# Holding each expert's weight loads back until the expert before has landed, in a one-layer hybrid block with 64 experts

## The chip, the cores and the metric

The kernel runs on one core of a Trainium2 chip. The metric is the device time of one execution in microseconds, the median of several. The core has TensorE (matmuls and transposes), VectorE, ScalarE, GpSimd and SyncE (SP), which issues DMAs; 16 DMA engines move data between HBM and the on-chip memory (SBUF). Engines run their own instruction streams and meet at semaphores.

## What is computed

One decoder layer over 512 tokens of width 1024, all in float32: an input projection, a spatial gating branch and an attention branch, an output projection, then a mixture of experts, and a gated per-layer embedding. The part that matters here is the mixture of experts:

```python
# t: 512 x 1024 tokens; 64 experts, hidden width 256, each token goes to 8 experts
scores = jax.nn.sigmoid((t @ w_router).astype(jnp.float32))
...
_, eidx = lax.top_k(jnp.where(emask, sel, -jnp.inf), TOP_K)
...
y = (jax.nn.silu(t @ w_sh_gate) * (t @ w_sh_up)) @ w_sh_down
for g in range(N_GROUPS):
    sl = slice(g * EXPERTS_PER_GROUP, (g + 1) * EXPERTS_PER_GROUP)
    a = jax.nn.silu(jnp.einsum('td,edf->tef', t, w_gate[sl])) * jnp.einsum('td,edf->tef', t, w_up[sl])
    y = y + jnp.einsum('tef,efd->td', a * combine[:, sl, None], w_down[sl])
```

The gate and up weights of one expert are 1024 x 256 each, the down weights 256 x 1024: three transfers of 1 MB for each of 64 experts.

## The kernel before

The projections and both branches come first, then the router and the shared expert, then a loop over the 64 experts, and a tail that sums eight expert rows for each token and applies the last gate.

**The expert loop.** Each expert handles up to 104 rows at once. GpSimd gathers its token rows from HBM by an indirect DMA (L621, `ya<-h_rows,gidx`, two buffers), TensorE transposes them (L1796), and runs gate and up as one product (L1767, L1775 to L1777), and the down product (L1811 to L1813). ScalarE and VectorE split each weight into a high and a low part before TensorE reads it (ScalarE L916 and VectorE L1370 for gate and up, ScalarE L935 and VectorE L1388 for down). GpSimd scatters the results back to HBM (L640, `expert_rows<-ya,sidx`). On TensorE step j does the gate and up product of expert j, the transposes of expert j+1 and the down product of expert j-1.

**The weight ring.** Weights lie in `arena`, a ring of `RING` = 4 slots; slot r holds gate, up and down of expert e with e mod 4 = r. All weight loads are issued by SP, on one queue, in program order. `expert_gu(e, r)` issues the gate and the up load (L422), and both count up the semaphore `w_gu[r]` by 16 as they land; `expert_dn(e, r)` issues the down load (L427) with `w_dn[r]`. Each of the 16 DMA engines moves its part of every transfer and adds 1. ScalarE waits for `w_gu` and `w_dn` before it splits a weight. SP loads experts 0 to 3 ahead of the loop. For experts 4 to 63 it waits for room: `gu_done`, which TensorE counts up after each gate and up product, and `dn_done`, after each down product:

```python
with sp.Fori(1, E // RING) as q:
    for r in range(RING):
        sp.wait_ge(gu_done, q * RING + (r - RING + 1))
        expert_gu(q * RING + r, r, one=False)
        sp.wait_ge(dn_done, q * RING + (r - RING + 1))
        expert_dn(q * RING + r, r, one=False)
```

With e = 4q + r, the gate and up loads of e wait until expert e-4 has left the products, and its down load until the down product of e-4 is done. Nothing on SP waits for a landing. As the down product of e-4 comes in TensorE's step e-3, after the gate and up product of e-3, one release lets three loads go together: down of e, gate and up of e+1. A second copy of this loop, L465 to L472, is for passes after the first.

Of the kernel before, what the change touches and what calls it, by code (L numbers as in the profile page):

```python
# [6 lines left out]
def hybrid_block_kernel(nc, a, out):  # L7
# [37 lines left out]
    E = a["w_router"].shape[2]  # L45
# [10 lines left out]
    RING = 4  # L56
# [12 lines left out]
    with ctx:  # L69
# [11 lines left out]
        def sem(name):  # L81
            return ctx.enter_context(nc.semaphore(name))
# [23 lines left out]
        def take(n):  # L106
# [73 lines left out]
              for i in range(2)]  # L180
# [34 lines left out]
        ROWS = [("positions", NT), ("g_mix", KD), ("g_ple_in", KD), ("sgu_b", G), ("mla_g_qa", KQ),  # L215
                ("mla_g_kva", KKV), ("qk_g_q_nope", 1), ("qk_g_k_nope", 1)]
        NROW = sum(n for _, n in ROWS)
        col = {}
        for name, n in ROWS:
            first = sum(len_ for _, len_ in ROWS[:len(col)])  # L220
            col[name] = sm[:, first:first + n]
# [58 lines left out]
        rt_logit, rt_score, m_ready = sem("rt_logit"), sem("rt_score"), sem("m_ready")  # L280
        rk_done, ks_done, rank_ready, R_ready, nb_ready = sem("rk_done"), sem("ks_done"), sem("rank_ready"), sem("R_ready"), sem("nb_ready")
        sh_gu, sh_silu, sh_a, sh_at, sh_aT, sh_dn, sh_y = (sem(f"sh_{n}") for n in ("gu", "silu", "a", "at", "aT", "dn", "y"))
        held = sem("held")
        xg_zero = sem("xg_zero")
        w_gu = [sem(f"w_gu{r}") for r in range(RING)]
        w_dn = [sem(f"w_dn{r}") for r in range(RING)]
# [77 lines left out]
        def _(sp):  # L364
# [54 lines left out]
            def expert_gu(e, r, one=True):  # L419
                for g, name in enumerate(("w_exp_gate", "w_exp_up")):  # L420
                    src = a[name][0][e] if one else a[name][0][bass.ds(e, 1)].rearrange("o d f -> (o d) f")
                    sp.dma_start(arena[:, r * WEXP + g * KD * FF:r * WEXP + (g + 1) * KD * FF],  # L422
                                 src.rearrange("(p k) f -> p (k f)", p=P)).then_inc(w_gu[r], 16)

            def expert_dn(e, r, one=True):
                src = a["w_exp_down"][0][e] if one else a["w_exp_down"][0][bass.ds(e, 1)].rearrange("o d f -> (o d) f")
                sp.dma_start(arena[:, r * WEXP + WGU:(r + 1) * WEXP],  # L427
                             src.rearrange("(p k) f -> p (k f)", p=P)).then_inc(w_dn[r], 16)
# [28 lines left out]
            with sp.Fori(1, E // RING) as q:  # L457
                for r in range(RING):
                    sp.wait_ge(gu_done, q * RING + (r - RING + 1))
                    expert_gu(q * RING + r, r, one=False)  # L460
                    sp.wait_ge(dn_done, q * RING + (r - RING + 1))
                    expert_dn(q * RING + r, r, one=False)
            sp.wait_ge(nb_ready, 1)
            n_pass = sp.value_load(nb_i, min_val=1, max_val=NPASS_MAX)
            with sp.If(n_pass > 1):  # L465
                with sp.Fori(1, n_pass) as b:
                    with sp.Fori(0, E // RING) as q:
                        for r in range(RING):
                            sp.wait_ge(gu_done, b * E + q * RING + (r - RING + 1))
                            expert_gu(q * RING + r, r, one=False)  # L470
                            sp.wait_ge(dn_done, b * E + q * RING + (r - RING + 1))
                            expert_dn(q * RING + r, r, one=False)  # L472

            sp.wait_ge(gate_room, n_pass)
# [1403 lines left out]
```

## Time and profile before

| | |
|---|---|
| median of 3 runs | 1344.4 us (1340.31 to 1345.1) |
| the profiled execution | 1339.67 us, of which span 1337.9 us |
| TensorE busy | 1197.0 us, 89% of the span |
| VectorE busy | 869.1 us, 65% |
| ScalarE busy | 720.0 us, 54% |
| GpSimd busy | 295.8 us, 22% |
| moved by DMA | 302.91 MB, mean 226 GB/s |

The span runs from the first to the last instruction of one execution taken by the profiler. Busy shares are averages over stages with different limits. The expert loop fills the time from about 540 to about 1225 us.

### The profile page before, as it was taken

The numbers are of one execution on the slowest core, as the hardware profiler recorded it, in microseconds if no ns is written. First come the engines' busy times: TensorE is split into PE (matmuls) and PEld (weight loads), VectorE is DVE, ScalarE is ACT, GpSimd is POOL, SyncE is SP. The second block draws the span as 40 slices with busy tenths as digits, with TensorE's granted clock in tenths as the row PEclk, the third lists the DMA queues.
The fourth block names the chain that finished last, engine by engine and source line by source line (L and its number), as shares of the span: only waits on it lengthen the run. The fifth ranks groups of instructions, "written<-read, shape, count | busy, mean of one in ns | idle before, by whom it ended". The sixth has DMA issues, their size and how long they took to land.

```text
span 1337.9 us, 17977 instructions
## 1 busy us (share of the span) xinstructions
PE 1197.0 (89%) x5569; PEld 901.7 (67%) x5569; DVE 869.1 (65%) x1379; ACT 720.0 (54%) x1270; POOL 295.8 (22%) x309
## 2 busy tenths in 40 slices
PE   6996999998999998999999999999999999996258
PEld 6984788685667844677777677666667766664246
DVE  5356342385443354888888778777787888775974
ACT  5542242374432240677677666666776767665223
POOL 2015000060551001122222112212221221112640
PEclk9997999998999999899999999999999999998579
DMA  6332112023002474499999999999999999985741
GB/s 208 126 114 75 63 63 81 20 81 142 1 1 79 156 300 157 181 343 343 352 352 333 341 338 349 344 338 332 339 344 335 337 335 338 343 294 209 325 199 48
DMA packets 71756, 302.91 MB, mean 226 GB/s; under 512 B 15107, under 2 KB 20262, under 8 KB 45734
## 3 DMA queue, kind: packets, MB, share of 16 engines
q1 hardware_dynamic: 51846, 264.64, 54.5%
q0 software_dynamic: 19296, 35.69, 8.1%
q10 hardware_dynamic: 576, 2.10, 0.4%
q8 instruction: 21, 0.34, 0.1%
q14 instruction: 17, 0.14, 0.0%
HBM read 290.64 MB, written 33.55 MB: 242 GB/s over the span
## 4 chain that ended last, share of the span: by engine, by line
PE 48%; DMA 30%; DVE 11%; issue 5%; ACT 4%; POOL 1%; SPq 1%; DVEq 0%; POOLq 0%; ACTq 0%
DMA arena<-in_w_exp_up 18%; DMA ya<-h_rows,gidx 11%; PE bank L1483 7%; PE bank L1518 5%; PE bank L1519 5%; PE bank L1522 5%; DVE resid L1433 2%; PE bank L1475 2%; PE bank L1796 2%; PE bank L1586 2%; DVE arena_r L1388 2%; PE bank L1767 2%; PE bank L1671 2%; PE bank L1583 1%; PE bank L1603 1%
## 5 line engine op out<-in xcount | busy, mean ns | idle before, releaser
L1370 DVE TENSOR_TENSOR arena_r<-arena,win_r 128x1024 fp32r<-128x1024 f32 x192 | 223.6, 1220 | 88.4 <-ACT win_r L916 88.3
L916 ACT ACTIVATE win_r<-arena 128x1024 fp32r<-128x1024 f32 x192 | 189.7, 1060 | 149.7 <-DMA arena<-in_w_exp_up 139.0
L640 POOL DMA_INDIRECT expert_rows<-ya,sidx x64 | 71.9, 1123 | 508.0 <-DVE gidx L1329 479.3
L1775 PE MATMUL bank<-win_r,work_r 128*128 128x512 f32 x384 | 176.8, 460 | 0.0
L1388 DVE TENSOR_TENSOR arena_r<-arena,hT_r 128x1024 fp32r<-128x1024 f32 x128 | 150.8, 1219 | 12.0 <-ACT hT_r L935 11.9
L1776 PE MATMUL bank<-win_r 128*128 128x512 f32 x384 | 150.1, 391 | 0.0
L1777 PE MATMUL bank<-arena_r,work_r 128*128 128x512 f32 x384 | 150.0, 391 | 0.0
L1518 PE MATMUL bank<-arena_r,hT_r 128*128 128x512 f32 (+2 forms) x320 | 123.6, 386 | 12.4 <-DVE win_r L1029 12.4
L935 ACT ACTIVATE hT_r<-arena 128x1024 fp32r<-128x1024 f32 x128 | 129.2, 1071 | 0.0
L1767 PE MATMUL bank<-arena,work 128*128 128x512 f32 x256 | 122.8, 602 | 1.6 <-ACT work L926 1.6
L1519 PE MATMUL bank<-arena_r 128*128 128x512 f32 (+2 forms) x320 | 122.3, 382 | 0.0
L1522 PE MATMUL bank<-win_r,hT_r 128*128 128x512 f32 (+2 forms) x320 | 122.0, 381 | 0.0
L1811 PE MATMUL bank<-hT_r,work_r 128*128 128x512 f32 x256 | 106.4, 416 | 1.8 <-DVE work_r L1363 1.8
L1029 DVE SCALAR_TENSOR_TENSOR win_r<-win,small,arena_r 128x512 fp32r<-128x512 f32 (+2 forms) x80 | 67.2, 909 | 62.3 <-ACT arena_r L693 62.3
L1813 PE MATMUL bank<-arena_r,work_r 128*128 128x512 f32 x256 | 101.1, 395 | 0.0
L1812 PE MATMUL bank<-hT_r,work_r 128*128 128x512 f32 x256 | 100.1, 391 | 0.0
L621 POOL DMA_INDIRECT ya<-h_rows,gidx x66 | 81.8, 1240 | 60.7 <-DVE gidx L1329 40.1
L1796 PE MATMUL bank<-ident,ya 128*128 128x128 f32 x512 | 70.5, 281 | 27.1 <-DMA ya<-h_rows,gidx 27.0
L1775 PEld LDWEIGHTS bank<-win_r,work_r 128*128 128x128 f32 x384 | 72.5, 189 | 28.6 <-issue 15.6
L1776 PEld LDWEIGHTS bank<-win_r 128*128 128x128 f32 x384 | 72.5, 189 | 28.6 <-issue 15.6
L1777 PEld LDWEIGHTS bank<-arena_r,work_r 128*128 128x128 f32 x384 | 72.2, 188 | 16.0
L1518 PEld LDWEIGHTS bank<-arena_r,hT_r 128*128 128x128 f32 x320 | 61.3, 191 | 26.4 <-DVE win_r L1029 16.5
(280 smaller groups left out, 2233.6 us busy)
## 6 DMA issues: line engine op xcount, KB each, us to landing
arena<-in_w_exp_gate SPq DMA_DIRECT2D x64, 1024.0 KB, 10.7
arena<-in_w_exp_up SPq DMA_DIRECT2D x64, 1024.0 KB, 25.1
arena<-in_w_exp_down SPq DMA_DIRECT2D x64, 1024.0 KB, 18.6
win<-in_w_in SPq DMA_DIRECT2D x8, 2048.0 KB, 7.7
arena<-expert_rows SPq DMA_DIRECT2D x8, 2048.0 KB, 11.9
win<-in_w_o SPq DMA_DIRECT2D x2, 2048.0 KB, 7.7
arena<-in_w_ple_gate SPq DMA_DIRECT2D x2, 2048.0 KB, 17.4
win<-in_mla_w_qb SPq DMA_DIRECT2D x4, 576.0 KB, 4.0
```

The lines of the kernel that those rows point to most:

```text
L916: act.activation(gu_hi[n % 2][:, :, cols], gu_w[n % RING][:, :, cols], ACT.Copy).then_inc(gu_hi_r, 1)
L935: act.activation(wdn_hi[j % 2][:, k, :], wdn[j % RING][:, k, :], ACT.Copy).then_inc(dn_hi, 1)
L1370: dve.tensor_tensor(gu_lo[n % RING][:, :, cols], gu_w[n % RING][:, :, cols], gu_hi[n % 2][:, :, cols].bitcast(F32), ALU.subtract).then_inc ...
L1388: dve.tensor_tensor(wdn_lo[j % RING][:, k, :], wdn[j % RING][:, k, :], wdn_hi[j % 2][:, k, :].bitcast(F32), ALU.subtract).then_inc(dn_lo, 1)
L1518: pe.matmul(b_, x_hi, w_hi, start=(k == 0), stop=False)
L1519: last = pe.matmul(b_, x_lo, w_hi, start=False, stop=False)
L1522: last = pe.matmul(b_, x_hi, w_lo, start=False, stop=(k == KD - 1))
L1767: pe.matmul(b_, x_f[:, k - KS, :], wgu[j % RING][:, k], start=(k == KS), stop=False)
L1775: pe.matmul(b_, x_hi[:, k, :], w_hi, start=False, stop=False)
L1776: pe.matmul(b_, x_lo[:, k, :], w_hi, start=False, stop=False)
L1777: last = pe.matmul(b_, x_hi[:, k, :], gu_lo[j % RING][:, :, k * FF:(k + 1) * FF], start=False, stop=(k == KS - 1))
L1811: pe.matmul(b_, hi, w_hi, start=(k == 0), stop=False)
```

## The change

SP's loop gets two more waits for each expert. Before the gate and up loads of expert e it waits until those of e-1 have landed (`w_gu` of the slot before, 32 counts for each use of the slot), and before the down load of e until that of e-1 has landed (`w_dn`, 16 counts). The waits for room stay. Between the two waits stands a count on a new semaphore, `room_seen`, for which nobody waits. When a load is issued, at most one down load (before gate and up), or one gate and one up load (before down), can still be on its way, so that at most three are outstanding. The same edit is made in the loop for further passes, which is cut here.

```diff
-        held = sem("held")
+        held, room_seen = sem("held"), sem("room_seen")
...
             with sp.Fori(1, E // RING) as q:
                 for r in range(RING):
                     sp.wait_ge(gu_done, q * RING + (r - RING + 1))
+                    sp.sem_inc(room_seen, 1)
+                    sp.wait_ge(w_gu[(r - 1) % RING], q * 32 + 32 * (r > 0))
                     expert_gu(q * RING + r, r, one=False)
                     sp.wait_ge(dn_done, q * RING + (r - RING + 1))
+                    sp.sem_inc(room_seen, 1)
+                    sp.wait_ge(w_dn[(r - 1) % RING], q * 16 + 16 * (r > 0))
                     expert_dn(q * RING + r, r, one=False)
```

On SP's stream at the start of the loop body (slot 0, then the start of slot 1) the rows are these. REGISTER_ALU and ISA are small instructions of the sequencer that carry the waits; `w_gu3` and `w_dn3` are the semaphores of slot 3, which holds the expert before.

```order
 L457 UNCONDITIONAL_BRANCH
 L457 ISA
-L422 ISA [waits gu_done]
+L461 REGISTER_ALU [waits gu_done]
+L422 ISA [waits w_gu3]
 L422 DMA arena<-in_w_exp_gate 128x2048
 L422 DMA arena<-in_w_exp_up 128x2048
-L427 DMA arena<-in_w_exp_down 128x2048 [waits dn_done]
+L465 REGISTER_ALU [waits dn_done]
+L427 DMA arena<-in_w_exp_down 128x2048 [waits w_dn3]
 L459 REGISTER_ALU
```

The order of the three loads is as it was; each wait for room now stands on an instruction of its own, and the wait for the landing behind it. On the same stream in slots 2 and 3 of the loop body:

```order
+L422 ISA [waits gu_done,w_gu1]
 L422 DMA arena<-in_w_exp_gate 128x2048
 L422 DMA arena<-in_w_exp_up 128x2048
-L427 DMA arena<-in_w_exp_down 128x2048 [waits dn_done]
-L422 ISA [waits gu_done]
+L427 DMA arena<-in_w_exp_down 128x2048 [waits dn_done,w_dn1]
+L422 ISA [waits gu_done,w_gu2]
```

Here both waits stand on the same instruction; no load has moved past another.

## Rows read from the trace of the kernel before

**Rows 1.** The page: the span, and the chain that ended last, by line.

```profile
span 1337.9 us, 17977 instructions
...
DMA arena<-in_w_exp_up 18%; DMA ya<-h_rows,gidx 11%; PE bank L1483 7%; PE bank L1518 5%; PE bank L1519 5%; PE bank L1522 5%; DVE resid L1433 2%; PE bank L1475 2%; PE bank L1796 2%; PE bank L1586 2%; DVE arena_r L1388 2%; PE bank L1767 2%; PE bank L1671 2%; PE bank L1583 1%; PE bank L1603 1%
```

**Rows 2.** Stretches: us, busy time (x count) by engine, granted clock, DMA share, GB/s.

```profile
546.80:734.60 187.80, 181.37 (x876) 136.78 (x875) 156.57 (x238) 137.91 (x221) 44.23 (x35) 1.00 0.94 336
734.60:1179.80 445.20, 414.86 (x1970) 308.47 (x1969) 349.26 (x534) 305.29 (x493) 94.48 (x82) 1.00 0.95 339
```

**Rows 3.** SP's own waits, 735 to 1191 us: total, times, longest.

```profile
SPq L427 <- PE bank L1813: 388.8, 42, 12.1
```

**Rows 4.** Up loads of experts 4, 6, 22, 22 to 63, and 63: issue, landing.

```profile
L422 SPq DMA_DIRECT2D arena<-in_w_exp_up x1: 376/376/376, 547.2 to 547.2; - x1
...
DMA to landing us min/median/max: 7.4/7.4/7.4
...
L422 SPq DMA_DIRECT2D arena<-in_w_exp_up x1: 381/381/381, 569.5 to 569.5; - x1
...
DMA to landing us min/median/max: 13.6/13.6/13.6
...
735.06 26.79 DMA arena<-in_w_exp_up
...
DMA to landing us min/median/max: 23.5/26.0/28.0
...
L422 SPq DMA_DIRECT2D arena<-in_w_exp_up x1: 381/381/381, 1180.3 to 1180.3; - x1
...
DMA to landing us min/median/max: 25.9/25.9/25.9
```

**Rows 5.** Waits of the engines, 734 to 1181 us: total, times, longest.

```profile
ACT win_r L916 <- DMA arena<-in_w_exp_up: 125.7, 41, 5.1
```

**Rows 6.** Gate loads, from issue to the 16th count: expert 4, experts 22 to 63.

```profile
DMA to landing us min/median/max: 4.8/4.8/4.8
...
DMA to landing us min/median/max: 9.6/10.7/14.0
```

**Rows 7.** The chain at a landing, and SP's next issue in the timeline.

```profile
1227.61 3.84 DMA expert_rows<-ya,sidx
...
1231.52 0.82 SPq L487 DMA_DIRECT2D arena<-expert_rows  x2
```

**Rows 8.** Issues and landings: up 38; down 4, down 21 to 63, down 38.

```profile
909.00 0.38 SPq L422 DMA_DIRECT2D arena<-in_w_exp_up  x1
...
DMA to landing us min/median/max: 27.5/27.5/27.5
...
DMA to landing us min/median/max: 5.5/5.5/5.5
...
DMA to landing us min/median/max: 16.4/19.3/20.1
...
919.59 0.33 SPq L427 DMA_DIRECT2D arena<-in_w_exp_down  x1
...
DMA to landing us min/median/max: 19.2/19.2/19.2
```

**Rows 9.** Gathers (L621), issue to landing: at 553.3, 572 to 735, 734 to 1181 us.

```profile
DMA to landing us min/median/max: 6.0/6.0/6.0
...
DMA to landing us min/median/max: 12.0/12.8/13.2
...
DMA to landing us min/median/max: 10.6/12.3/13.2
```

**Rows 10.** The chain in the first stretch: start us, us, what.

```profile
696.35 13.19 DMA ya<-h_rows,gidx
...
717.48 12.63 DMA ya<-h_rows,gidx
```

More of the change, by code:

```diff
@@ L469, in _ @@
                             sp.wait_ge(gu_done, b * E + q * RING + (r - RING + 1))
+                            sp.sem_inc(room_seen, 1)
+                            sp.wait_ge(w_gu[(r - 1) % RING], b * (32 * E // RING) + q * 32 + 32 * (r > 0))
                             expert_gu(q * RING + r, r, one=False)
                             sp.wait_ge(dn_done, b * E + q * RING + (r - RING + 1))
+                            sp.sem_inc(room_seen, 1)
+                            sp.wait_ge(w_dn[(r - 1) % RING], b * (16 * E // RING) + q * 16 + 16 * (r > 0))
                             expert_dn(q * RING + r, r, one=False)
```

## The prediction

> **What bounds the kernel now.** I begin with the page. The chain that ended last is nearly one half TensorE, but the one wait in it that is worth more than a matmul line is the landing of the experts' up weights, 18% of the span, with the gather of token rows next at 11% [rows 1]. Both lie in the loop over 64 experts. So the second view is the table of stretches over that loop, cut at the issue of experts 4, 22 and 63 (gate loads at 546.8, 734.6 and 1179.8 us). In the first stretch 18 experts go by in 187.8 us, 10.43 us each, in the second 41 in 445.2 us, 10.86 us each. TensorE is busy 181.37 / 18 = 10.08 and 414.86 / 41 = 10.12 us per expert, at a granted clock of 1.00 in both, which is the 2.4 GHz level. The DMA engines are busy 94 to 95% of both stretches [rows 2]. Two resources stand almost level, and the loop goes from one pace to another along the way. The question is which of them sets the second pace.
>
> The waits seem to speak for TensorE: in the second stretch SP stands 388.8 us, 42 times, at L427, until TensorE has finished the down product of four experts back [rows 3]. SP is never late; it waits for room. But a wait for room tells nothing of where the things that fill the room are. That is in the landings. Expert 4's up load, issued at 547.2, lands 7.4 us later; expert 6's, at 569.5, after 13.6; expert 22's, at 735.06, after 26.79; from there on the median is 26.0, and the last one, at 1180.3, takes 25.9 [rows 4]. In the first stretch the weights are issued every 10.43 us and pile up in the queues. From the landings themselves: 583.1 (569.5 + 13.6) to 761.9 for experts 6 to 22 is 11.2 us each, and 761.9 to 1206.2 for experts 22 to 63 is 10.84 us each. So the transfers land at about 11 us per expert all along. TensorE was ahead for some 18 experts, used up the four-slot ring, and has gone at the transfers' pace since. ScalarE confirms it, as it waits 125.7 us in 41 times for the up load in the second stretch, 3.1 us per expert [rows 5]. Queued weights, not slots or TensorE, bound the loop.
>
> One more thing must be read from the landings. The gate load is issued just ahead of the up load and shares its semaphore, and what stands as its landing is the 16th of 32 counts. In an empty queue it comes after 4.8 us and in the steady loop after 10.7 [rows 6], when the up load's last count needs 26.0 more or less. Engines that went in step would put one transfer of some 3 us between the two. So a part of the 16 DMA engines has done its share some 15 us before the rest: the load is bound by a few laggards, whose queues never run dry, while the quick ones wait for the next issue.
>
> **The change, part by part.** For each of the 60 experts of SP's loop two waits and two counts on SP are added; no transfer, byte, tile or compute instruction changes. SP stands in waits for nearly nine tenths of the second stretch (388.8 of 445.2 us), so the instructions themselves cost nothing; if SP's time ever counted, they would be under the 0.4 us that a load's issue takes [rows 4], and the gap below allows 0.3 us for them. Behind the waiting instruction on SP's queue stand only the later weight loads and, after the last, the load of the last gate's weights and of the expert rows. GpSimd's gathers and scatters have their own queue and pass.
>
> Which of the two waits will come last? Room is given three experts before the need: expert 38's up load is issued at 909.00 and lands 27.5 us later, at 936.5, when expert 35's slot is long free. So in the bound state the new wait ends last and SP issues by landings. The gate and up loads of e go out when those of e-1 have landed, with the down load of e-1 still in flight; the down load of e goes out when that of e-1 has landed, with gate and up of e in flight. The order of transfers on each DMA engine stays the same. The depth falls from the 26 us of work that lay ahead of a new load to one to three transfers.
>
> The laggards decide. Does their queue run dry? What must be covered is the way from the last count of the up load, through SP, to the first bytes of the next. SP reacts at once: the scatter's landing at 1227.61 + 3.84 = 1231.45 lets an SP load go at 1231.52 [rows 7]. For issue, first byte and receipt I take the lightly loaded rows: gate landed after 4.8 us [rows 6] and the up load behind it at 547.2 + 7.4 = 554.6, which is 3.0 us later, so 4.8 - 3.0 = 1.8 us is fixed; a lone down load takes 5.5 us [rows 8], and 5.5 - 3.0 = 2.5. With 0.3 us for SP the gap to cover is 2.1 to 2.8 us (an estimate from these rows). The cover at the tighter of the two places is the one down load still queued. It lands after its up load by 919.59 + 19.2 - 936.5 = 2.3 us at expert 38 [rows 8], and by the medians 10.6 + 19.3 - 26.0 = 3.9 us; a third of 10.84 is 3.6. At the other place two transfers cover, some 7 us, and nothing is lost.
>
> So the price per expert lies between 0 (2.1 against 3.9) and 0.5 us (2.8 against 2.3). A second effect lies inside this: backlogs average out when one engine or another is late, and the landings do scatter, 23.5 to 28.0 us for the up load around 26.0 [rows 4]; with a depth of one transfer each such delay makes all the others wait. Against it, the laggards have other work in a gap: a gather takes 12.8 and 12.3 us to land under weights and 6.0 us with almost none in flight [rows 9], so for most of each period rows of gathers and scatters are pending and can use a gap. I take a loss of 0.25 us at one expert in three, 0.08 us on average, nearer to the low end, since the medians clear the gap; 58 experts x 0.08 = 4.6 us. All else is kept: early on, experts 4 and 5 find the queues as empty as now; the tail after the last landing at 1206.2, 131.7 us, has the same work; TensorE's 10.1 us per expert lie beside the transfers.
>
> A rule of the Trainium skill speaks against the change: DMA: Bandwidth & Descriptors, section "Anatomy of one DMA", puts a fixed cost of about 2.0 us on a transfer, most of it until the write is confirmed, and a transfer held for a landing pays it in series. The rows above show 1.8 to 2.5 us, so trace and page agree; by the page's 2.0 alone the cover of 2.3 to 3.9 us would hold and the price be nil.
>
> **Sum.** The profiled execution took 1339.7 us (span 1337.9 and 1.8 around it), the median of the three runs is 1344.4. 1339.7 + 4.6 = 1344.3 for such an execution, 1344.4 + 4.6 = 1349 against the median.
>
> **The rivals.**
>
> (a) The queues do run dry (slower). It is the same mechanism at the high price: a gap at every expert. At 0.5 us it is 58 x 0.5 = 29 us, 1373 us. It decides from the point where the way from landing to first byte exceeds the time that the laggard has left in its down load, about 3.2 us on average between 2.3 and 3.9. For it: the scatter of the landings, and that only one transfer covers. Against it: medians and the pending gather rows. If the cover failed altogether, it would be 58 x 2.5 = 145 us; I see nothing for that, as the down load is always behind.
>
> (b) A shallow queue makes the laggards or the gathers quicker (faster). Gathers count too: in the first stretch the chain runs through gathers of 13.19 and 12.63 us, one per two experts, 696.35 to 717.48 being 21.1 us [rows 10]. If the weights fell under 10.43 us per expert, the loop would run at the first stretch's pace to its end: 41 x (10.86 - 10.43) = 18 us, 1327 us; if the gathers shortened too, TensorE's 10.1 would be next, 59 x 0.33 = 19 us more, 1307 us. For it: the gather's 6.0 against 12.8. Against it: the laggards are never without weights in either version, the same bytes pass, and the landings' pace was already 11.2 us when the depth was still 13.6 us, no better than at 26. A word of the skill bears on the gathers: the same page's section "Queues, rings and completion order" says that an engine takes turns between queue rows a packet at a time, by which a gather would wait for the neighbour's turn at any depth and not get quicker; no row here shows turns, and the chances don't use it.
>
> (c) The wait never ends last, so nothing changes: 1344. That would need landings earlier than room. Only at experts 4 to 6 is that so.
>
> **How the numbers follow.** What a measurement of this kernel can tell from no change is about 0.5%, 6.7 us. My forecast of about 1349 (0 to 0.11 us per expert) has 0.42 together with (c), which is 0.02 of it. Losses above that, to 0.5 us, 1351 to 1373, have 0.30, and beyond 0.06. Gains, (b), have 0.22: 0.14 down to 1325 and 0.08 beyond. The range takes the forecast, (a) to a little over its 0.5 us and (b) as far as 18 us: 1324 to 1374; outside are 0.08 + 0.06 and some slack. The likeliest case alone is 1340 to 1351. Faster 0.22, same 0.42, slower 0.36.
>
> **What the profile after would show.** SP's waits move: from L427 on TensorE's L1813 to waits on the up and down loads. The up load's issue-to-landing falls from 26 to about 10 us (11 less what SP waits), the down load's to about 10 too, and gate's 16th count comes 1 to 3 us, not 15, before the up load's last. The distance between issues stays 10.8 to 11.0 us in the second stretch; 11.3 would be rival (a), 10.4 rival (b). ScalarE still waits some 3 us per expert for the up load. The gathers stay above 11 us; under 9 speaks for (b). DMA busy share stays 93 to 95%; under 91% is (a). The forecast is wrong if the laggards are not the same few engines all along, since then a shared stop at each landing costs what the backlog now hides, or if a deep backlog itself slows them.

## The result

The changed kernel takes 1368.52 us (median of 4 runs, 1362.5 to 1373.34) against 1342.36 us before (4 runs, 1340.15 to 1345.1). The ratio is 1.0192, 95% interval 1.0142 to 1.0242: 26 us slower. That lies inside the stated range but outside the forecast of about 1349; it falls in the zone of rival (a), 1351 to 1373.

The page of the changed kernel, span and the chain that ended last, by line:

```profile
span 1368.9 us, 18157 instructions
...
DMA arena<-in_w_exp_up 47%; PE bank L1491 7%; PE bank L1526 5%; PE bank L1527 5%; PE bank L1530 5%; DVE resid L1441 2%; PE bank L1483 2%; PE bank L1594 2%; SPq L422 2%; PE bank L1679 2%; PE bank L1591 2%; PE bank L1611 1%; DVE arena_r L1436 1%; DVE win_r L1037 1%; PE bank L1602 1%
```

The landing of up weights was 18% of the chain [rows 1] and is 47% now. The gathers, 11% before, are gone from it. The table of stretches, cut at the same issues as in [rows 2] (gate loads of experts 4, 22 and 63):

```profile
551.10:760.90 209.80, 197.14 (x942) 146.56 (x941) 166.94 (x256) 145.14 (x236) 45.44 (x39) 1.00 0.89 316
760.90:1224.10 463.20, 420.87 (x1969) 309.73 (x1968) 348.81 (x532) 304.37 (x493) 92.74 (x83) 0.99 0.92 325
```

An expert takes 209.8 / 18 = 11.66 us and 463.2 / 41 = 11.30 us; it was 10.43 and 10.86. The last two columns matter: the DMA engines are busy 0.89 and 0.92 of the time instead of 0.94 and 0.95, and move fewer GB/s. So more of their time is idle than before. SP's waits in the second stretch, where [rows 3] had 388.8 us for room:

```profile
SPq L422 <- DMA arena<-in_w_exp_up: 327.7, 42, 10.3
SPq L427 <- DMA arena<-in_w_exp_down: 60.2, 38, 3.6
```

SP never waits for room there. From issue to landing in the same stretch, in this order up, gate (16th count), down, gather (L629) and scatter (L648):

```profile
DMA to landing us min/median/max: 8.3/10.7/12.6
...
DMA to landing us min/median/max: 5.3/7.5/9.0
...
DMA to landing us min/median/max: 8.5/11.2/14.5
...
DMA to landing us min/median/max: 6.6/10.6/14.1
...
DMA to landing us min/median/max: 4.6/6.7/11.1
```

The queues are as shallow as the change says: the up load lands after 10.7 us instead of 26.0. The gather comes down from 12.3 to 10.6 us.

The trace also has the time of each single count. For experts 24 to 61 (38 of them, medians of each rank), the 16 counts of a down load come in the kernel before at 5.2 to 5.7 us after its issue for the first eight, and then at 6.4, 9.3, 11.1, 11.5, 13.9, 16.5, 18.8 and 19.3 us. So half of the DMA engines have next to no backlog, and the other half has one of very unequal length. In the changed kernel the 16 counts come between 8.1 and 11.2 us. From gate's 16th count to the up load's last it is 15.9 us before and 3.4 us in the changed kernel.

**Where the 31 us of the two profiled executions lie** (1370.64 and 1339.67). Expert 4's gate load is issued at 551.1 instead of 546.8, so 4.3 us were lost before the loop. Of these, 3.1 us are SP's wait at L433, ahead of all expert loads, which is 92.4 us here and 89.3 us before. They are not the change's: in the experiments' profiles, whose code is the same up to there, this wait lies anywhere between the two. The other 1.2 us were not traced. From the landing of expert 4's up weights to that of expert 63's it is 558.8 to 1236.4 against 554.6 to 1206.2, 677.6 against 651.6 us: 26.0 us, 0.44 us for each of 59 experts. After that 132.5 against 131.7. The loss is the loop's, and it is spread over all of it.

### The profile page after: what moved, and what is told of

The parts are those of the page before. It is cut to its first block, busy times and chain, and to the rows that moved or that the text cites. A ratio compares the mean times of both kernels' runs of the same rounds, so it can differ in the third digit from the quotient of the medians.

```text
span 1368.9 us, 18157 instructions
## 1 busy us (share of the span) xinstructions
PE 1207.8 (88%) x5569; PEld 904.3 (66%) x5569; DVE 868.7 (63%) x1379; ACT 717.5 (52%) x1270; POOL 290.9 (21%) x309
## 4 chain that ended last, share of the span: by engine, by line
DMA 47%; PE 38%; DVE 8%; SPq 2%; issue 2%; ACT 2%; POOL 1%; ACTq 0%; DVEq 0%; POOLq 0%
DMA arena<-in_w_exp_up 47%; PE bank L1491 7%; PE bank L1526 5%; PE bank L1527 5%; PE bank L1530 5%; DVE resid L1441 2%; PE bank L1483 2%; PE bank L1594 2%; SPq L422 2%; PE bank L1679 2%; PE bank L1591 2%; PE bank L1611 1%; DVE arena_r L1436 1%; DVE win_r L1037 1%; PE bank L1602 1%
## 5 line engine op out<-in xcount | busy, mean ns | idle before, releaser
L648 POOL DMA_INDIRECT expert_rows<-ya,sidx x64 | 72.1, 1127 | 538.0 <-DVE gidx L1337 495.8
L1784 PEld LDWEIGHTS bank<-win_r 128*128 128x128 f32 x384 | 72.8, 190 | 29.0 <-issue 15.9
L629 POOL DMA_INDIRECT ya<-h_rows,gidx x66 | 77.4, 1173 | 60.8 <-DVE gidx L1337 40.3
L1526 PEld LDWEIGHTS bank<-arena_r,hT_r 128*128 128x128 f32 x320 | 61.5, 192 | 26.4 <-DVE win_r L1037 16.5
## 6 DMA issues: line engine op xcount, KB each, us to landing
arena<-in_w_exp_up SPq DMA_DIRECT2D x64, 1024.0 KB, 10.7
arena<-in_w_exp_down SPq DMA_DIRECT2D x64, 1024.0 KB, 11.2
```

The source lines that it names most:

```text
L1526: pe.matmul(b_, x_hi, w_hi, start=(k == 0), stop=False)
L1784: pe.matmul(b_, x_lo[:, k, :], w_hi, start=False, stop=False)
```

## The experiments

All ratios are to the kernel before, timed on the same chip. The second copy of SP's loop, for further passes, isn't run with these inputs.

**Which stop costs: gu_only and dn_only.** Each takes one of the two holds out of the first-pass loop: gu_only keeps the hold for gate and up, dn_only that for down.

```diff
 gu_only, against the changed kernel
                     sp.wait_ge(dn_done, q * RING + (r - RING + 1))
-                    sp.sem_inc(room_seen, 1)
-                    sp.wait_ge(w_dn[(r - 1) % RING], q * 16 + 16 * (r > 0))
 dn_only, against the changed kernel
                     sp.wait_ge(gu_done, q * RING + (r - RING + 1))
-                    sp.sem_inc(room_seen, 1)
-                    sp.wait_ge(w_gu[(r - 1) % RING], q * 32 + 32 * (r > 0))
```

Expected of gu_only: 

> Only the gate and up loads wait for a landing (of those of the expert before); the down load goes out when there is room. Theory 1 (shared stop: in each period another of the loaded DMA engines is last, and at a landing all the others have at most one down load left, so the period becomes the longest of 16 instead of the pace of the steadily slowest): the stop at the gate and up landing is the costly one and stays, 18 to 26 us over before. Theory 2 (dry queue: it is always the same laggard, and the way from the last count to the first byte is longer than its one down load): same place, same price, 20 to 26 us. Theory 3 (each of the two stops costs its share): about half, 10 to 15 us.

Expected of dn_only: 

> Only the down load waits for the landing of the down load before; gate and up go right behind it, so two to five transfers are outstanding and two cover each stop. Theory 2 (dry queue) says no loss, within 2 us of before. Theory 1 (shared stop) says that a stop with two transfers of slack costs little, 0 to 8 us. Theory 3 (each stop its share) says 10 to 15 us.

Measured: gu_only 1367.84 us, ratio 1.0194 (1.0135 to 1.0253), the whole loss. dn_only 1338.3 us, ratio 0.9970 (0.9944 to 0.9997), no loss, even a trifle faster. So the stop for gate and up, behind which one down load is queued, costs everything, and the one behind which gate and up are queued costs nothing. The third theory is out.

**How deep: two_back.**

```diff
-                    sp.wait_ge(w_gu[(r - 1) % RING], q * 32 + 32 * (r > 0))
+                    sp.wait_ge(w_gu[(r - 2) % RING], q * 32 + 32 * (r > 1))
...
-                    sp.wait_ge(w_dn[(r - 1) % RING], q * 16 + 16 * (r > 0))
+                    sp.wait_ge(w_dn[(r - 2) % RING], q * 16 + 16 * (r > 1))
```

> Both holds stay, but for the landing of the expert two back: up to six transfers outstanding, at least four at each issue. Theory 1 and theory 2: nearly nothing left of the loss, 0 to 5 us over before; issue to landing of the up load about 20 us, the distance of issues 10.8 to 10.9. If waiting for landings itself were the cost (more instructions, a slower start of a load), all 26 us would stay.

Measured: 1335.32 us, ratio 0.9944 (0.9927 to 0.9962). The loss is gone and there is a gain of 0.6%, which was not expected. This kernel has the same added waits and counts, so neither they nor waiting for landings as such is the cost.

**Is the queue dry at each stop: late_issue and later_issue.** The gate load is issued later on purpose; 8 and 24 counts on SP.

```diff
                     sp.wait_ge(w_gu[(r - 1) % RING], q * 32 + 32 * (r > 0))
+                    for _ in range(8):          # 24 in later_issue
+                        sp.sem_inc(room_seen, 1)
```

Expected of late_issue: 

> The changed kernel with eight more counts on SP between the landing and the issue of the gate load, some 0.6 to 0.7 us. Theory 2 (dry queue, the gap is already past its cover at every expert): the delay is paid in full, 59 x 0.65 = 38 us more than the changed kernel, 64 us over before. Theory 1 (shared stop): paid by those periods in which the engine that was last also has little left, half of it or so, 12 to 30 us more, 40 to 55 us over before. If the down load covers the stop altogether: no more than the changed kernel, 26 us over before.

Expected of later_issue: 

> The changed kernel with 24 more counts on SP between the landing and the gate load, about 2.1 us. With 0.65 us the period of an expert rose by 0.12 us only, so I now hold: theory 1 (shared stop), the chain of weights passes through a stop in about one period of five, where an engine starts late and is last next time. By it the longer delay uses up the cover of the one down load and the price is convex: 0.8 to 1.5 us more per expert than the changed kernel, 47 to 90 us, so 75 to 115 us over before. Rival, theory 3: the stop costs something else than idle time, and delays stay nearly free: under 30 us more than the changed kernel.

Measured: late_issue 1374.12 us, ratio 1.0203 (1.0139 to 1.0267); later_issue 1369.07 us, ratio 1.0188 (1.0149 to 1.0226). Neither differs from the changed kernel. That the delay was there shows the chain. Two up loads and the gate issue between, first of the changed kernel:

```profile
808.20 8.96 DMA arena<-in_w_exp_up
...
817.31 0.33 SPq L422
...
817.74 10.70 DMA arena<-in_w_exp_up
```

and of later_issue (start us, us, what):

```profile
808.19 9.77 DMA arena<-in_w_exp_up
...
819.55 0.33 SPq L422
819.97 9.86 DMA arena<-in_w_exp_up
```

Landing to issue is 817.31 - 817.16 = 0.15 us in the one and 819.55 - 817.96 = 1.59 us in the other, 1.44 us more in each of 59 periods, 85 us of delay in all. In late_issue the chain has an up load landing at 821.10 and the gate issue at 821.74, 0.64 us, so the delay added there is 0.49 us, 29 us in all. None of it is in the time. Theory 2, by which each stop already pays for a dry queue, falls: it wanted the delays paid in full. Theory 1 in the form that I gave it falls with it, as far as its price for a delay goes (47 to 90 us).

The packets in the trace say more. For experts 24 to 61, no packet of a weight load is under way on any engine for some time around the next gate issue in 37 of 38 experts of later_issue, 0.6 us in the median and up to 1.1; in the changed kernel this happens once in 38. So in later_issue the weight queue does run dry on all engines, and it costs nothing more. What is under way then are rows: averaged over experts 24 to 59, in the half microsecond that starts 2.0 us after the up load's landing, packets of weights take 0.2 of the 16 engines and packets of gathers and scatters 8.4. In the kernel before they take 15.2 and 1.1 at the same place. The gathers of later_issue, 780 to 1180 us, land much sooner than the changed kernel's 10.6 us:

```profile
DMA to landing us min/median/max: 5.3/6.5/9.4
```

So the rows go through in the gap, and the weights behind them are less disturbed. That this repays the delay is a reading of these numbers; no run separates it. What the profiles show beside it is in the rows of the weights' queue on the page (packets, MB, their time as a share of 16 engines' span), of the changed kernel:

```profile
q1 hardware_dynamic: 51846, 264.64, 53.0%
```

and of later_issue, whose span is 1370.1 us:

```profile
q1 hardware_dynamic: 51846, 264.64, 51.6%
```

The same packets took 0.530 x 1368.9 = 725.5 us per engine in the one and 0.516 x 1370.1 = 707.0 in the other; before it was 54.5% of 1337.9, 729.2 us. So the hold did not make transfers slower, and in later_issue they were quicker. That these 18.5 us per engine pay a part of the delay back is not shown; the profile does not say which packets are the laggard engines'.

**Who is late: spread, spread_held and spread_two.** The slot number of a token row is permuted, so that the valid rows of a gather and a scatter (64 of 104 on average: 512 tokens to 8 of 64 experts) lie over all partitions, where they filled them from 0 up. spread has no holds, spread_held both, spread_two those of two_back.

```diff
-            pool.iota(iota[:, :], pattern=[[1, NPASS_MAX * NS + P]], base=0, channel_multiplier=0,
+            nb_ = NPASS_MAX * NS + P - 24
+            pool.iota(iota[:, nb_:], pattern=[[1, 24]], base=nb_, channel_multiplier=0,
+                      allow_small_or_imprecise_dtypes=True)
+            pool.iota(iota[:, 0:nb_].rearrange("p (b i j) -> p b i j", i=13, j=8), pattern=[[NS, nb_ // NS], [1, 13], [13, 8]],
+                      base=0, channel_multiplier=0,
```

Expected of spread: 

> The kernel before (no holds), with the slots of each expert numbered otherwise: ranks go to partitions 0, 8, 16 and so on in turn instead of filling partitions from 0 up, so that the some 64 valid rows of a gather and a scatter lie over all of the 104 partitions. The same sums, in other rows. If the laggard engines are those that carry the rows of gathers and scatters, the load evens out, the landings' pace falls from 10.84 to TensorE's or the gathers' 10.1 to 10.4 us, and the up load's issue to landing to 10 to 15 us: 18 to 35 us under before. If the laggards are slow for another reason, no change, within 4 us.

Expected of spread_held: 

> The changed kernel (both holds) with the same spread of rows. Theory 1 (shared stop among loaded engines): with all engines loaded alike and less than the laggards were, the period falls to 10.3 to 10.8 us, 5 to 25 us under the changed kernel's 11.36 x 60, but it stays 5 to 20 us above the spread kernel without holds. If evenness were all that the loss needs, it would equal the spread kernel within 4 us; if the rows play no part, it equals the changed kernel.

Expected of spread_two: 

> The spread of rows with the holds of two experts back. If spread alone frees the loop from its laggards, the depth no longer matters and this equals the spread kernel within 4 us. If the gain of 8 us that the two-back hold showed comes from shorter gathers or less crowding, it adds some 2 to 8 us to the spread kernel's gain.

Measured: spread 1296.88 us, ratio 0.9655 (0.9622 to 0.9688); spread_held 1294.01, 0.9648 (0.9591 to 0.9704); spread_two 1295.45, 0.9639 (0.9603 to 0.9674). The stretch from 800 to 1100 us, columns as in [rows 2], of spread:

```profile
800.00:1100.00 300.00, 296.88 (x1440) 224.37 (x1439) 256.23 (x391) 225.74 (x360) 72.53 (x60) 1.00 1.01 367
```

of spread_held:

```profile
800.00:1100.00 300.00, 300.00 (x1457) 227.10 (x1456) 261.52 (x399) 229.19 (x366) 76.50 (x61) 1.00 0.99 371
```

TensorE is busy 297 and 300 of 300 us, and 367 and 371 GB/s pass where there were 339 in the second stretch [rows 2]. All three take 3.5% less than the kernel before, and over 5% less than the changed kernel. This shows that the laggards' lateness in the kernel before comes from where the gathered and scattered rows lie. The load is more even now, but not even: in spread the 16 counts of a down load come between 5.3 and 16.2 us after issue, where they came between 5.2 and 19.3 (medians of each rank, experts 24 to 61). With the rows spread the holds cost nothing that can be measured. But TensorE bounds the loop there, so it would hide a price, and the comparison of spread with spread_held can't tell whether uneven engines are needed for the loss.

**The price of a delay with the rows spread: spread_late.** The 24 counts in spread_held.

> The kernel with spread rows and both holds, with the 24 more counts between the landing and the gate load, 1.4 us as measured before. With all engines loaded alike, the way from landing to first byte (2.1 + 1.4 us) is longer than the one down load (2.5 to 3.3 us). Theory 1 (idle engines on the path cost their time): 0.4 to 1.0 us more per expert than 9.9, of which TensorE's 10.1 hides 0.2: 12 to 45 us over the spread kernel with holds. Rival (a delay is given back, since transfers run quicker for it, as in the two delayed kernels with uneven rows): within 5 us of it.

Measured: 1339.94 us, ratio 0.9977 (0.9941 to 1.0014), 46 us over spread_held, 0.78 us per expert for a delay of 1.44. So with the rows spread a delay is paid, where with the rows in the low partitions it was free. The weights' queue, spread_held (span 1291.8) and spread_late (span 1346.1):

```profile
q1 hardware_dynamic: 51846, 264.64, 54.4%
```

```profile
q1 hardware_dynamic: 51846, 264.64, 51.9%
```

702.7 and 698.6 us per engine: here the delay brought next to no relief, 4 us, and cost 46.

**Three outstanding, but two behind each stop: fine.** Gate and up count on semaphores of their own, and each load waits for its own kind.

```diff
+                    if held is not None:
+                        sp.wait_ge((w_g, w_u)[g][(r - 1) % RING], held)
...
-                    sp.wait_ge(w_gu[(r - 1) % RING], q * 32 + 32 * (r > 0))
-                    expert_gu(q * RING + r, r, one=False)
+                    expert_gu(q * RING + r, r, one=False, held=q * 16 + 16 * (r > 0))
```

> Gate and up have semaphores of their own, and each of the three loads waits for its own kind of the expert before: gate(e) for gate(e-1), up(e) for up(e-1), down(e) for down(e-1). Still at most three transfers outstanding, but two, not one, lie behind each stop. If the price comes from the stop behind which only one down load is queued (theories 1 and 2), it goes: within 5 us of before, perhaps under it as the down-only and two-back holds were. If three outstanding are too few whatever the order (too little in flight), it stays at 20 us or more.

Measured: 1336.33 us, ratio 0.9938 (0.9918 to 0.9958). It is not the number outstanding that costs, but what lies behind the stop: with gate and up issued together after a stop, one transfer is still queued; with each issued by itself, there are two. SP's waits of this kernel over the whole span show that the holds did bind (total, times, longest):

```profile
SPq L425 <- DMA arena<-in_w_exp_up: 211.3, 57, 6.1
SPq L425 <- DMA arena<-in_w_exp_gate: 146.5, 54, 4.9
SPq L430 <- DMA arena<-in_w_exp_down: 120.3, 50, 5.1
```

**One fixed laggard: marked and marked_held.** A transfer of 17 rows of 4 KB, HBM to HBM, is added ahead of each gate load, without holds and with both.

```diff
+                    sp.dma_start(mark_dram[bass.ds((q * RING + r) * 17, 17), :], a["w_in"][0][0:17, 0:D]).then_inc(marked, 16)
                     expert_gu(q * RING + r, r, one=False)
```

Expected of marked: 

> The kernel before with one more transfer per expert, 17 rows of 4 KB from HBM to HBM ahead of the gate load, which by its 17 rows runs on one DMA engine alone. This makes one and the same engine the laggard of every period. Expected 2 to 3 us more per expert if that engine is one of the loaded ones (120 to 180 us over before), 0 to 60 us if it has slack. It is the base for the next run.

Expected of marked_held: 

> The same one-engine transfer in the changed kernel, ahead of the gate load and behind the wait, so that the cover of the stop is one down load as in the changed kernel. Theory 1 (who is last changes from period to period, the chain hops to an engine that started late): with one engine always last there is no hop and the hold costs nothing, within 8 us of the marked kernel without holds. Theory 2 (way longer than cover for the same engine): the hold costs its 26 us here too. If the hold made transfers crowd or slowed the laggard itself, also 26 us or more.

Measured: marked 1458.28 us, ratio 1.0859 (1.0821 to 1.0897); marked_held 1452.75 us, 1.0805 (1.0776 to 1.0834). Where the added transfer makes a laggard of its own, the same hold with the same one down load behind its stop costs nothing. The counts show that there is one laggard: in marked, 15 of the 16 counts of a down load come within 5.9 to 8.4 us of its issue and the last after 26.0 us (medians of each rank), and for these 4 MB more the kernel takes 115 us more. But the pair does not separate the theories as it was meant to. The down load lands 3.4 us after its up load there (median of the 19 experts between 24 and 61 of which marked_held's trace has all counts, 2.8 to 4.2), and 2.5 us after it in the changed kernel. So the cover is about 0.9 us longer, and theory 2, by which a short cover is what costs, would expect no loss either. The up load's issue to landing, 780 to 1180 us, in marked_held:

```profile
DMA to landing us min/median/max: 10.3/10.9/11.8
```

It scatters over 1.5 us, and in the changed kernel, with nearly the same median, over 4.3 us (8.3 to 12.6). The loss does not simply go with this scatter, though. In the same window later_issue, with the whole loss, and spread_held, with none, have these:

```profile
DMA to landing us min/median/max: 8.2/9.3/10.4
...
DMA to landing us min/median/max: 8.1/9.3/11.5
```

## Where the prediction held and where it failed

**What bounds the kernel**: right. The landings' pace bound the loop; laggard DMA engines set it. The counts of the down loads and the spread runs show that, and that TensorE's 10.1 us stand right behind. The number was inside the range only because the range took in rival (a), to which I gave 0.30; the forecast itself, 1349, was 20 us low.

**The new wait ends last, SP issues by landings**: right, 42 of 42 times for gate and up in the second stretch, and 38 of 42 for down. Place and kind of the loss, the stop for gate and up with one down load behind it, were named, and gu_only and dn_only confirm the place. The cost of the added instructions was nil as said: two_back has the same ones.

**The step that failed** is "The laggards decide. Does their queue run dry?", and with it the 0.08 us per expert. I compared one way (2.1 to 2.8 us) with one cover (2.3 to 3.9 us), as if one engine were meant, and took a small loss for the tight places. The term measured 0.44 us, five times as much: 26.0 instead of 4.6 us.

Both sides of the comparison were off. The 3.9 us came from the medians of two loads and from the issue distance of a single expert. Taken expert by expert from the counts (24 to 61), the down load lands 2.3 to 4.5 us after its up load in the kernel before, 2.7 in the median, and 2.3 to 4.8 in the changed kernel, 2.5 in the median. So the medians did not clear the gap as I wrote. The way was overestimated: in later_issue, where the queue does run dry, the first weight packet on any engine starts 1.0 us (median) after the gate load's issue, and the last one ends 0.5 us before the down load's last count. With SP's 0.15 us that makes an estimate of about 1.7 us. Engines that start later than the first have a longer way, and the profile does not say how much longer.

The widest margin at the stop in the changed kernel, from SP's timeline:

```profile
919.95 0.37 SPq L422 DMA_DIRECT2D arena<-in_w_exp_up  x1
921.83 0.33 SPq L427 DMA_DIRECT2D arena<-in_w_exp_down  x1
928.38 0.33 SPq L422 DMA_DIRECT2D arena<-in_w_exp_gate  x1
```

The up load, with a landing of 8.3 us, is down at 928.2, the next gate load goes at 928.38, and the down load lands 11.2 us after its issue, at 933.0, 4.8 us after the up load. That is the longest of the 38. A usual one has its up load issued at 1018.86 and landed after 10.8 us, and the down load landed at 1032.24, 2.6 us after that. By the estimate of 1.7 us even this covers the way on the engine that starts first; how it stands on the others the profile does not say.

So it is shown where the loss arises (the stop for gate and up, gu_only), that a second transfer behind that stop removes it (fine, two_back), and that a still longer and visibly dry gap adds nothing to it (later_issue). It is not shown why one transfer behind the stop costs 0.44 us per expert. Theory 1 is one argument: the loaded engines' shares of rows come at different moments, and another engine is last in each period. Without holds each evens out its bad periods in its backlog. With a stop that leaves one transfer, engines that were ahead go idle and can't use their lead in their next bad period. I had this effect in the text ("each such delay makes all the others wait") and priced it inside the 0.08, and the prediction's last line named its condition, laggards that are not the same few engines. The runs don't settle it. The counts show several engines with a long backlog (16.5, 18.8 and 19.3 us for the last three), which it needs. But it priced the delays at 12 to 30 and 47 to 90 us and they cost nothing, marked and marked_held fit theory 2 as well, and the scatter of the landings does not follow the loss. No run follows a single engine, and why the stop costs what it does stays open.

The prediction sets the skill's 2.0 us beside the 1.8 to 2.5 us of its rows. The Trainium skill, DMA: Bandwidth & Descriptors, section "Anatomy of one DMA", gives that figure for transfers issued from GpSimd, while the loads held here are issued by SP; the packets of later_issue give the 1.7 us above for these.

**Pending gather rows fill the gaps**: they did not prevent the loss, but the packets show them at work. In the changed kernel, in the half microsecond that starts 0.5 us after the up load's landing, rows take 4.4 of the 16 engines and weights 5.3, where they take 0.7 and 15.5 before; in later_issue rows take over half of the engines while weights take almost none. "The laggards are never without weights in either version" was wrong for later_issue's gap, and in the changed kernel some engines are without work at the stop. The gather did shorten to 10.6 us, where I had said above 11.

**Rival (b)** had a true core on the small side. Holds that leave two or more transfers behind each stop gain 0.3 to 0.6% (dn_only, two_back, fine); where that gain comes from is not shown. The sentence on the landings' pace, 11.2 at a depth of 13.6 us, "no better than at 26", compared two stretches with different traffic and was too weak to exclude it.

**The signs.** Issues 11.30 us apart: rival (a)'s 11.3. DMA share 0.92: between the two marks that I set (93 to 95%, or under 91%). Gate's 16th count comes 3.4 us before the up load's last; I had said 1 to 3. ScalarE waits for the up load

```profile
ACT win_r L924 <- DMA arena<-in_w_exp_up: 151.5, 41, 5.8
```

3.7 us per expert instead of 3.1.

## What to carry to other kernels

When issues are held for landings, count what is still queued behind each stop, and not how many transfers are outstanding: here one transfer of 1 MB behind the stop cost 26 us, and two behind each stop, with the same three outstanding, gained 7. Compare cover and way within one expert, and not by the medians of two loads. Where a transfer's first and last counts lie far apart, look for what loads the engines unevenly before touching the order of issues: spreading the valid rows of the gathers over the partitions gave 3.5%, more than any hold.

## What was not expected of the hardware

- The rows of an indirect gather and scatter load the DMA engines by the partition they are in. With the valid rows in the low partitions half of the 16 counts of a down load came within 5.7 us and the last after 19.3, and the loop moved 339 GB/s; with the same rows spread it moved 367 to 371.
- A shorter backlog made the kernel a little quicker as long as two transfers lay behind each stop: dn_only, two_back and fine run 0.3 to 0.6% under the kernel before. Quicker packets don't explain it: the weights' queue took 54.9% of a span of 1331.7 us in two_back, 731 us per engine, and 55.4% of 1334.2 in fine, 739 us, against 729.2 before. In later_issue, which is slow, it took 707.0.
- A gap in the weights on every engine, 0.6 us in the median of later_issue, cost nothing with the rows in the low partitions. With the rows spread the same 1.44 us of delay cost 46 us.
- With a fixed laggard and no holds the issue itself is held. In marked, a gate load took SP 7.82 us to issue, where 0.33 is usual:

```profile
917.60 7.82 SPq L424 DMA_DIRECT2D arena<-in_w_exp_gate  x1
```

- SP's wait at L433, ahead of the loop, varies by 3 us between profiles whatever is done behind it: 89.3 us before, in two_back and in fine, 92.4 us in the changed kernel and in spread. Of the changed kernel:

```profile
SPq L433 <- POOL ya L601: 92.4, 1, 92.4
```
